# The expert layer's Gelu as a cubic on DVE and a tanh on ACT, with the gates weighed ahead of each round's search step

## What is computed

```
q = (xt @ w_query).reshape(T, H, 2, PEER_HALF)                 # H = 8 heads
s = einsum('thcd,cnd->thcn', q, sub_keys)                      # 2 x 128 keys
sv, si = lax.top_k(s, K)                                       # K = 16
cand_s = sv[:, :, 0, :, None] + sv[:, :, 1, None, :]           # 256 pairs
top_s, pos = lax.top_k(cand_s, K)
idx = the pair's expert number, one of 16384
gate = softmax(top_s)
a = einsum('thkd,td->thk', down[idx], x)                       # 1024 long dot products
c = gate * gelu(a)                                             # tanh form of the gelu
out = einsum('thk,thkd->td', c, up[idx])
```

## Time and profile before

| | us |
|---|---|
| runs | 2218.52, 2218.03, 2214.88 |
| median | 2218.03 |
| profiled execution, its time | 2219.33 |
| its span, first to last instruction | 2217.6 |
| outside the span | 1.7 |
| DVE busy | 1292.8 (58% of the span) |
| PE busy | 1985.1 (90%) |
| ACT busy | 632.7 (29%) |
| POOL busy | 611.9 (28%) |

### The profile page before, as it was taken

How to read it: one execution, slowest core, us unless ns; L and a number is a source line. 1 busy time by engine, 2 the same in 40 slices (tenths; PEclk the granted TensorE clock), 3 DMA queues, 4 the chain that set the end, 5 groups by cost and what they waited for, 6 DMA issues and landing times.

```text
span 2217.6 us, 19179 instructions
## 1 busy us (share of the span) xinstructions
PE 1985.1 (90%) x6132; PEld 1069.0 (48%) x6132; DVE 1292.8 (58%) x3377; ACT 632.7 (29%) x1518; POOL 611.9 (28%) x560
## 2 busy tenths in 40 slices
PE   7999999899999899888889988898989899778777
PEld 5885587588644344443334443443434444223322
DVE  5550264200033568786576877657687757777764
ACT  2000134200024332543142255223235423222221
POOL 1100010000000233343343333334334434444442
PEclk9999999999999999999999999999999999999999
DMA  9998734444676899999999999999999999999997
GB/s 393 420 409 313 262 127 141 169 152 151 237 272 215 319 420 421 421 421 410 421 421 420 421 418 412 405 419 421 419 404 404 416 418 407 422 421 418 421 420 317
DMA packets 110614, 793.89 MB, mean 358 GB/s; under 512 B 12394, under 2 KB 12522, under 8 KB 15674
## 3 DMA queue, kind: packets, MB, share of 16 engines
q0 software_dynamic: 79936, 581.08, 63.6%
q1 hardware_dynamic: 29088, 207.73, 24.9%
q10 hardware_dynamic: 1498, 3.99, 0.5%
HBM read 791.67 MB, written 4.75 MB: 359 GB/s over the span
## 4 chain that ended last, share of the span: by engine, by line
PE 53%; DMA 26%; DVE 11%; ACT 6%; issue 3%; POOL 1%; DVEq 0%; POOLq 0%; ACTq 0%
DMA wide<-experts_in,pick_idx 21%; PE PS L1517 17%; PE PS L1075 15%; PE PS L517 9%; PE PS L1591 6%; DMA ring<-experts_in,pick_idx 4%; DVE wide L1145 3%; PE PS L1797 1%; ACT diag L1061 1%; ACT L1056 1%; DMA early<-ada_in 1%; DVE topi L1093 1%; DVE topi L1096 1%; PE PS L1640 1%; PE PS L511 1%
## 5 line engine op out<-in xcount | busy, mean ns | idle before, releaser
L1075 PE MATMUL PS<-wide,diag 128*128 128x512 f32 x1824 | 880.6, 619 | 167.6 <-ACT diag L1061 160.1
L1220 POOL DMA_INDIRECT wide<-experts_in,pick_idx x456 | 516.4, 1132 | 1179.6 <-PE PS L1075 738.5
L1145 DVE CUSTOM_DVE_ANT_0 wide<-wide,htok 128x1024 f32<-128x1024 f32 x454 | 549.8, 1223 | 216.3 <-DMA wide<-experts_in,pick_idx 206.0
L1075 PEld LDWEIGHTS PS<-wide,diag 128*128 128x128 f32 x1824 | 343.1, 196 | 626.3 <-issue 353.7
L1517 PE MATMUL PS<-hT,ring 128*128 128x256 f32 x1648 | 361.8, 382 | 6.4 <-DMA ring<-wts_in 2.8
L1517 PEld LDWEIGHTS PS<-hT,ring 128*128 128x128 f32 x1648 | 315.2, 192 | 52.6 <-issue 7.3
L517 PE MATMUL PS<-ring,hTm 128*128 128x512 f32 (+1 forms) x704 | 323.3, 588 | 1.9 <-ACT hTm L478 0.8
L1061 ACT ACTIVATE diag<-cst,coef 128x128 f32<-128x128 f32 x510 | 177.0, 394 | 262.1 <-DVE coef L1168 259.1
L1056 ACT ACTIVATE coef<-dots 128x2 f32<-128x2 f32 x255 | 51.9, 204 | 587.6 <-DVE dots L1145 586.8
L517 PEld LDWEIGHTS PS<-ring,hTm 128*128 128x128 f32 x704 | 133.7, 192 | 163.0 <-issue 154.8
L1075 PE MATMUL PS<-ring,diag 128*128 128x512 f32 x224 | 113.0, 628 | 28.0 <-ACT diag L1061 27.9
(11 more groups left out here) (351 smaller groups left out, 1483.2 us busy)
## 6 DMA issues: line engine op xcount, KB each, us to landing
ring<-wts_in SPq DMA_DIRECT2D x191, 1024.0 KB, 4.8
early<-ada_in POOLq DMA_DIRECT2D x36, 1024.0 KB, 12.5
wide<-experts_in,pick_idx POOLq DMA_INDIRECT x456
ring<-wts_in SPq DMA_DIRECT2D x8, 780.0 KB, 4.1
strip_t<-strips_one POOLq DMA_DIRECT2D x1, 2048.0 KB, 20.4
strip_dil<-strips_one POOLq DMA_DIRECT2D x1, 1536.0 KB, 27.6
x<-x_in ACTq DMA_DIRECT2D x1, 1024.0 KB, 5.7
bias_t<-strip_t POOLq DMA_DIRECT2D x1, 1024.0 KB, 9.0
```

Of the source, the lines that this page charges most:

```text
L1075: last = pe.matmul(PS[:, SUMS[i] + half, :], diag[:, n % RING, :], ups(n)[:, half * BANK:(half + 1) * BANK], start=k == 0, stop=k == PICKS ...
L1145: v.tensor_tensor_reduce(out=downs(n), in0=downs(n), in1=htok[:, tb, :], scale=1.0, scalar=0.0, op0=ALU.mult, op1=ALU.add, accum_out=dots[ ...
L1220: pool.indirect_dma_start(row(n), None, experts.rearrange("l e d -> (l e) d"), bass.IndirectOffsetOnAxis(pick_idx[:, u % 4, k:k + 1], 0), ...
```

## The change

The Gelu in its tanh form is d/2 times (1 + tanh(B (d + A d^3))), with A = 0.044715 and B = the root of 2/pi. DVE now makes y = (A d d + 1) d in two operations (`gelu_in`, L1148 and L1149 of the changed file) and d times gate in a third (`half_gates`, L1152); the factor 0.5 sits in `gate`. ACT makes tanh(B y) in place of the Gelu, and `weigh` is one operation (tanh + 1) times `halves` (L1188). `weigh` stands ahead of the search step, where it stood behind it. ACT's semaphore `dots_done` now counts rounds, and comes from y. The two dots are waited for with the chain's counter.

```diff
--- before.py
+++ after.py
@@ -7,6 +7,8 @@
 
 
 from contextlib import ExitStack
+
+import math
 
 import numpy as np
 
@@ -51,6 +53,7 @@
 EXPERT_HEADS = 8
 NKEYS = 128
 K16 = 16
+GELU_A, GELU_B = 0.044715, math.sqrt(2.0 / math.pi)
 PICKS = EXPERT_HEADS * K16
 RING = 8
 ROWS = RING + 1
@@ -244,6 +247,8 @@
         pick_idx = sb("pick_idx", [P, 4, K16], U32, stack=two)
         gate = sb("gate", [P, 4, K16], stack=two)
         dots = sb("dots", [P, 2, ROUND], stack=two)
+        cube = sb("cube", [P, 2, 2, ROUND], stack=two)
+        halves = sb("halves", [P, 2, ROUND], stack=two)
         coef = sb("coef", [P, 2, 2, ROUND], stack=two)
         diag = sb("diag", [P, RING, P], stack=two)
 
@@ -1044,16 +1049,16 @@
                     rnd = u * ROUNDS + rr
                     if rnd + 1 == UNITS * LAYERS * ROUNDS:
                         for j in range(ROUND):
-                            act.wait_ge(m["dots_done"], rnd * ROUND + j + 1)
-                            act.activation(coef[:, 0, rr % 2, j:j + 1], dots[:, rr % 2, j:j + 1], ACT.Gelu_apprx_tanh)\
+                            act.wait_ge(m["dots_done"], rnd + j + 1)
+                            act.activation(coef[:, 0, rr % 2, j:j + 1], cube[:, 1, rr % 2, j:j + 1], ACT.Tanh, scale=GELU_B)\
                                 .then_inc(m["gelu_ready"], 1)
                             act.wait_ge(m["coef_ready"], rnd + j + 1)
                             act.wait_ge(m["ups_used"], rnd * ROUND + j + 1 - RING)
                             act.activation(diag[:, (rr * ROUND + j) % RING, :], ident, ACT.Copy, scale=coef[:, 1, rr % 2, j:j + 1])\
                                 .then_inc(m["diag_ready"], 1)
                         break
-                    act.wait_ge(m["dots_done"], rnd * ROUND + ROUND)
-                    act.activation(coef[:, 0, rr % 2, :], dots[:, rr % 2, :], ACT.Gelu_apprx_tanh).then_inc(m["gelu_ready"], 1)
+                    act.wait_ge(m["dots_done"], rnd + 1)
+                    act.activation(coef[:, 0, rr % 2, :], cube[:, 1, rr % 2, :], ACT.Tanh, scale=GELU_B).then_inc(m["gelu_ready"], 1)
                     act.wait_ge(m["coef_ready"], rnd + 1)
                     if rnd * ROUND >= RING:
                         act.wait_ge(m["ups_used"], rnd * ROUND + ROUND - RING)
@@ -1135,28 +1140,43 @@
                     e = topf[:, 128 + 32 * a:144 + 32 * a]
                     V(v.reduce_sum(topf[:, 224:225], e, AX.X))
                     V(v.reciprocal(topf[:, 224:225], topf[:, 224:225]))
-                    V(v.tensor_scalar(gate[:, g % 4, :], e, topf[:, 224:225], None, ALU.mult))
+                    V(v.tensor_scalar(gate[:, g % 4, :], e, topf[:, 224:225], 0.5, ALU.mult, ALU.mult))
+
+            def gelu_in(u, rr, j0, j1):
+
+                d, t, y = dots[:, rr % 2, j0:j1], cube[:, 0, rr % 2, j0:j1], cube[:, 1, rr % 2, j0:j1]
+                V(v.scalar_tensor_tensor(t, d, GELU_A, d, ALU.mult, ALU.mult))
+                v.scalar_tensor_tensor(y, t, 1.0, d, ALU.add, ALU.mult).then_inc(m["dots_done"], 1)
+
+            def half_gates(u, rr, j0, j1):
+                V(v.tensor_tensor(halves[:, rr % 2, j0:j1], dots[:, rr % 2, j0:j1],
+                                  gate[:, u % 4, rr * ROUND + j0:rr * ROUND + j1], ALU.mult))
 
             def dot(u, rr):
 
                 for j in range(ROUND):
                     n = u * K16 + rr * ROUND + j
                     v.wait_ge(rows_loaded[n % ROWS], 16 * (n // ROWS + 1))
-                    v.tensor_tensor_reduce(out=downs(n), in0=downs(n),
-                                           in1=htok[:, tb, :], scale=1.0, scalar=0.0, op0=ALU.mult,
-                                           op1=ALU.add, accum_out=dots[:, rr % 2, j:j + 1]).then_inc(m["dots_done"], 1)
+                    V.go(v.tensor_tensor_reduce(out=downs(n), in0=downs(n),
+                                                in1=htok[:, tb, :], scale=1.0, scalar=0.0, op0=ALU.mult,
+                                                op1=ALU.add, accum_out=dots[:, rr % 2, j:j + 1]))
+                V.done()
+                gelu_in(u, rr, 0, ROUND)
+                half_gates(u, rr, 0, ROUND)
 
             def last_round(u, rr):
                 for j in range(ROUND):
                     n = u * K16 + rr * ROUND + j
                     v.wait_ge(rows_loaded[n % ROWS], 16 * (n // ROWS + 1))
-                    v.tensor_tensor_reduce(out=downs(n), in0=downs(n),
-                                           in1=htok[:, tb, :], scale=1.0, scalar=0.0, op0=ALU.mult,
-                                           op1=ALU.add, accum_out=dots[:, rr % 2, j:j + 1]).then_inc(m["dots_done"], 1)
+                    V(v.tensor_tensor_reduce(out=downs(n), in0=downs(n),
+                                             in1=htok[:, tb, :], scale=1.0, scalar=0.0, op0=ALU.mult,
+                                             op1=ALU.add, accum_out=dots[:, rr % 2, j:j + 1]))
+                    gelu_in(u, rr, j, j + 1)
+                    half_gates(u, rr, j, j + 1)
                     v.wait_ge(m["gelu_ready"], u * ROUNDS + rr + j + 1)
                     v.wait_ge(m["diag_ready"], n - 2)
-                    v.tensor_tensor(coef[:, 1, rr % 2, j:j + 1], coef[:, 0, rr % 2, j:j + 1],
-                                    gate[:, u % 4, rr * ROUND + j:rr * ROUND + j + 1], ALU.mult).then_inc(m["coef_ready"], 1)
+                    v.scalar_tensor_tensor(coef[:, 1, rr % 2, j:j + 1], coef[:, 0, rr % 2, j:j + 1], 1.0,
+                                           halves[:, rr % 2, j:j + 1], ALU.add, ALU.mult).then_inc(m["coef_ready"], 1)
 
             def weigh(u, rr):
 
@@ -1165,7 +1185,7 @@
                 if rnd >= 2:
 
                     v.wait_ge(m["diag_ready"], ROUND * (rnd - 1))
-                v.tensor_tensor(coef[:, 1, rr % 2, :], coef[:, 0, rr % 2, :], gate[:, u % 4, rr * ROUND:(rr + 1) * ROUND], ALU.mult)\
+                v.scalar_tensor_tensor(coef[:, 1, rr % 2, :], coef[:, 0, rr % 2, :], 1.0, halves[:, rr % 2, :], ALU.add, ALU.mult)\
                     .then_inc(m["coef_ready"], 1)
 
             def sum_of(i):
@@ -1189,6 +1209,7 @@
                         opening()
                     if i and u == u0 and rr == 1:
                         sum_of(i - 1)
+                    weigh(u, rr)
                     if u + 1 == end:
                         if beside and rr < 4:
                             search(end, 2 * rr)
@@ -1199,7 +1220,6 @@
                         search(u + 1, rr + 4)
                     elif u + 2 < end:
                         search(u + 2, rr - 4)
-                    weigh(u, rr)
                     if beside:
                         beside.to(2 * ((u - u0) * ROUNDS + rr) + 1)
             if not beside:
```

## The result

The changed kernel takes 2230.36 us in the median of five runs (2226.78 to 2232.79); the kernel before, on the same chip, 2217.3 (2214.88 to 2218.52). The ratio is 1.0055, with a 95% interval of 1.0042 to 1.0069: slower by 13.1 us. That lies inside the range of 2210 to 2231, at its upper edge, but the forecast's likeliest case was no change. The profiled execution took 2232.2 us, with a span of 2230.5.

The account below looks back on a forecast made before the run. The prediction took the DMA to bound the kernel from 750 to 2200 us. DMA stage 0 (ends -4.6 and +5) and end +0.5 turned the profiled 2219.33 into 2219.8, a median of 2218.5; range 2210 to 2231.

Parts of the forecast that it names:

- rival B: Dense parts of the three mixers: DVE becomes the bound, 15 us slower in all, 2233; chance 0.24 together with C.
- C: ACT's table loads stay or come back elsewhere, leaving only the new work; ends like rival B, chance 0.24 shared with it.
- main case: Whole kernel: DMA stage unchanged, end 0.5 us longer, median 2218.5, within 2213.6 to 2222.5; chance 0.66.
- The bound: From the 14th of forty slices on, the DMA is nine tenths busy or more; the change moves no byte.
- closing the dips: Filling the DMA's slack moments from 750 to 2200 us by earlier row release: at most 13.8 us, really 4.6.
- DVE's price: Between dots and search: three operations add 122 us busy time; with standstill 0.75 us a round, 191 us in all.
- ACT's relief: On ACT, 81 table loads of 1283 ns go, 104 us; ACT is not what the stage ends on.
- What covers it: DVE's idleness, 331 us, covers 191; from 850 to 1000 us, 151 us of need in 150, level.
- The queue as a reserve: In each dense part, the queue of issued rows lends a microsecond and gets it back after.
- The signs that it named: Trace readings to tell the cases apart: DMA share and rate, DVE and ACT busy time, waits for rows and before weighing.
- Rival A: DMA stage: earlier `diag` spreads PE's bursts and the DMA never slackens; 2213 to 2205, chance 0.10.
- The end: Last pick, after the last byte: dots to weighing takes longer with nothing to hide it, +0.5 us.

Follow-up runs that it names:

- the best version found: The kernel before with weighing taken off DVE and done on ACT in two small copies: 2216.94 against 2218.98 us, ratio 0.9989.

## Why the prediction was partly right

The range holds the result only because it took in the price of rival B, to which, with C, the prediction gave 0.24; its main case, no change at 0.66, did not come true.

*The bound.* Right on the whole. From the 15th slice on the DMA is again nine tenths busy in every slice but the last, and the best version found gains 2 us, under the 4.6 us that the prediction allowed for closing the dips. (It read the DMA as full from the 14th slice on; that one has 8 tenths and 319 GB/s, and nothing hangs on it.) In the dense parts of the mixers the DMA was full only as long as DVE was in time.

*DVE's price.* Right. It said 0.75 us a round; the trace has 0.77 to 0.80. It said 122 us of added work; the three groups have 41.1 + 41.0 + 40.3 = 122.4 us. DVE's busy time as a whole rose by 109.6, as `halves` runs half beside the operation ahead of it (2067.94 against 2067.86). That `half_gates` fills most of the tanh trip was wrong: 0.26 us of idleness remain behind it. The waits for rows were to fall from 238 to about 100 us; they fell to 107.4 + 14.5 = 121.9.

*ACT's relief.* Right in number (81 loads, 107 us), half right in worth. Nothing alone, about 10 us where DVE is short: without it the same operations cost 20.7 us. The Trainium skill (ScalarE: Activation LUTs, "What ACT_TABLE_LOAD costs") adds a drain of about 1380 ns to each load. The changed kernel's trace doesn't show it either: the load at 939.07 takes 1.28 us, and its function starts at 940.37. ACT's busy time fell by 107.0 us (632.7 to 525.7), 81 loads of 1.283 us being 103.9.

*What covers it.* This step failed. The prediction added 19 us of need in 850 to 1000 us to a stretch with 22 us of idleness, took it that 4 of the 15.5 us before weighing would remain, and called the result, 151 us for 150, level. Measured, 13.3 us of waiting before weighing remain, against 15.5 before. Of these, 24 rounds at 0.26, 6.2 us, are the tanh trip itself, which is in the 0.77. The other 7.1 are real waits for ACT in the three rounds shown above, not the 4 that the sum had: the search step used to cover part of such a wait, and the new place of weighing takes that cover away. (With weighing behind the search, the same three rounds wait 2.01, 3.34 and 0.80 us, 6.1 in place of 7.9.) With 7.1 the prediction's own sum is 150 - 22 + 19 + 7 = 154 us for 150. DVE got through 24 rounds where it had been 25. In 1650 to 1750 us 16 rounds were done instead of 18. The forecast took a stretch that needs all of its time for one that holds.

*The queue as a reserve.* Also short of the mark: the prediction let the queue lend a microsecond and get it back. Where DVE lags far enough, PE arrives late at a seam of the mixer, is slow for a few microseconds, and all nine buffers are held: 215 and 139 GB/s in 5 us. Of the 11.9 us that the DMA lost more than before, 7.3 lie in the six worst stretches and 4.6 in a lower rate elsewhere. That the seam is what turns DVE's lag into lost time is argued from these rows, not shown by a run of its own.

*The signs that it named.* Those of B came: 414 and 389 GB/s in the two dense parts, where it said below 415, and 105.7 us of idleness before weighing, where it said above 60. That second sign was badly placed, as the forecast's own trip of 0.27 us makes 69 us in 255 rounds. The wait before `weigh` is 0.26 us in most rounds, not 0.1.

*Rival B* is what happened, at 13 us where it gave 15, though by rows it lost most in two of the three mixers (slices 17 and 19, 31 and 32). Its chance of 0.24 was too low: a sum that ends within 1 us of full in 150 us, with a price per round uncertain by a quarter of a microsecond (25 x 0.25 = 6 us), is no evidence for the side of no change.

*Rival A* had no part in it. *The end:* the cubic's 0.5 us there lies below what these runs can tell, and wasn't tried alone.

The Trainium skill's warning about small operations (VectorE: DVE Perf Modes, "The TRN2 errata") pointed at the right cost. The 58 cycles of its table would have given an estimated 48 us of work. The rows have 160 ns an operation, before and after, which agrees with what the page says below that table: the fixed term measures about 150 cycles, at 0.96 GHz an estimated 0.16 us.

What stays open is how the 4.3 us between the changed kernel and that with weighing behind divide between the 0.19 to 0.22 us of longer standstill in most rounds and the late rounds that the search no longer covers; their intervals overlap.

## What to carry to other kernels

- In a stage that the DMA bounds, another engine's idleness is a stock that is held in places, not a mean. Add the price per round to each dense stretch by itself; where the sum comes within a per cent or two of the stretch, as 151 us for 150 here, don't forecast that it holds.
- Price a step on an engine from the end of its input to the start of the next thing it does, standing still included. Two elements cost 0.16 us of work and 0.19 us chained, and moving work to another engine is no gain if the first one waits for it (two operations fewer, 42 us slower).
- Taking work off an engine pays only where somebody waits for it: 81 table loads were worth 0 or 10 us, by the state of another engine.

## Not expected

- A small DVE operation that isn't made to wait for the last one starts 0.08 us behind its start (2067.86 to 2067.94), one that waits starts 0.19 us behind (2067.67 to 2067.86). Here independence more than halved the price of such an operation.
- After a lag, PE restarts at a granted clock of 0.65 or 0.66 in the mean of 5 us, which is the lower of its two levels (1.2 of 2.4 GHz) for part of them, just when it is the engine that all wait for: three picks took 8.05 us there, and the same three took 5.42 us in the kernel before.
